# Routing tokens tile by tile inside the cross-attention projection, 5 and 6 weight homes, and filler products, in a one-core decoder block

## What is computed

```python
def rmsnorm(x, g):
    y = xf * lax.rsqrt(jnp.mean(xf * xf, axis=-1, keepdims=True) + EPS)
    return (y * g).astype(x.dtype)

x = x + hybrid_mixer(rmsnorm(x, mix_norm_g[l]), ...)            # 512 x 1024
x = x + cross_attention(rmsnorm(x, xatt_norm_g[l]), mem_n, ...) # ends with o @ w_xo
x = x + hierarchical_moe(rmsnorm(x, ffn_norm_g[l]), ...)
return rmsnorm(x, final_norm_g)

def hierarchical_moe(h, ...):
    g_logits = t @ w_group + b_group                    # 4 groups, the best one is taken
    g_idx = jnp.argmax(g_logits, axis=-1)
    e_logits = (t @ w_router + b_router)                # 4 experts of that group, the best two
    top_v, top_i = lax.top_k(softmax(e_sel), 2)         # their weights, renormalised
    hid = silu(t @ w_gate[e]) * (t @ w_up[e])           # 1024 -> 256
    out = out + (hid * combine[e]) @ w_down[e]          # 256 -> 1024
```

## Time and profile before

| | us |
|---|---|
| median of 3 runs (744.43 to 748.34) | 744.91 |
| the profiled execution | 748.57 |
| its span in the trace | 746.8 |
| PE busy | 695.0 |
| PE in the chain that ended last | 89% of the span |

### The profile page before, as it was taken

The page is one execution under the profiler, slowest core; times in us unless marked ns, Lnnn a source line. Parts: engine busy times, 40 slices in busy tenths (PEclk is TensorE's granted clock), DMA queues, the critical chain, the costliest instruction groups (busy, mean ns, idle before and its releaser), DMA issues.

```text
span 746.8 us, 8354 instructions
## 1 busy us (share of the span) xinstructions
PE 695.0 (93%) x3388; PEld 332.9 (45%) x3388; DVE 279.4 (37%) x647; ACT 147.9 (20%) x305; POOL 69.5 (9%) x94
## 2 busy tenths in 40 slices
PE   5999999999999899999999999999946999999975
PEld 4744444454455565444444446444432333333322
DVE  3108699925143564313220016312241821212147
ACT  3010431004262343311000014201110010101002
POOL 2000090520100000000000000000010010100122
PEclk9999999999999999999999999999966999999988
DMA  8703330303130203300029311200196999999552
GB/s 296 271 0 113 113 112 2 112 2 113 57 117 23 91 1 113 114 0 1 0 83 367 112 59 54 112 30 28 64 355 207 323 351 389 369 388 352 204 185 112
DMA packets 65715, 108.21 MB, mean 145 GB/s; under 512 B 5401, under 2 KB 40461, under 8 KB 65677
## 3 DMA queue, kind: packets, MB, share of 16 engines
q1 hardware_dynamic: 62796, 97.19, 37.3%
q0 software_dynamic: 2880, 10.49, 3.9%
HBM read 98.23 MB, written 9.44 MB: 144 GB/s over the span
## 4 chain that ended last, share of the span: by engine, by line
PE 89%; DVE 5%; ACT 2%; DMA 1%; another core or an unknown queue 1%; issue 1%; POOL 1%; DVEq 0%; POOLq 0%
PE bank L1742 25%; PE bank L2043 15%; PE bank L1614 12%; PE bank L1752 6%; PE bank L1642 6%; PE bank L1774 2%; PE bank L2116 2%; PE bank L1788 2%; PE bank L2096 2%; PE bank L1560 2%; PE bank L1596 2%; PE bank L1983 2%; PE bank L1959 1%; PE bank L1859 1%; PE bank L1884 1%
## 5 line engine op out<-in xcount | busy, mean ns | idle before, releaser
L1742 PE MATMUL bank<-hT,W 128*128 128x512 f32 x368 | 159.7, 593 | 0.9 <-DVE hT L1006 0.9
L2043 PE MATMUL bank<-W,n_sb 128*128 128x512 f32 x256 | 111.5, 594 | 0.7 <-ACT n_sb L974 0.7
L1742 PEld LDWEIGHTS bank<-hT,W 128*128 128x128 f32 x368 | 69.4, 190 | 87.5 <-issue 86.0
L2043 PEld LDWEIGHTS bank<-W,n_sb 128*128 128x128 f32 x256 | 48.1, 190 | 59.8 <-issue 58.3
L1614 PE MATMUL bank<-W,A 128*32 128x512 f32 x528 | 73.2, 614 | 1.5 <-DVE A L1160 1.5
L1319 DVE SCALAR_TENSOR_TENSOR A<-A,pc 128x511 f32<-128x511 f32 (+29 forms) x60 | 51.6, 860 | 2.0
L1642 PE MATMUL bank<-Dn,A 128*32 128x512 f32 x384 | 46.5, 627 | 5.1 <-ACT A L775 5.1
L649 POOL TENSOR_TENSOR rstd<-ss,mhalf 128x1 f32<-128x1 f32 x14 | 7.7, 549 | 376.5 <-DVE ss L990 376.5
L1614 PE MATMUL bank<-hT,A 128*32 128x512 f32 x96 | 42.3, 594 | 0.0
L1507 DVE TENSOR_TENSOR x_sb<-x_sb,bank 128x512 f32<-128x512 f32 x16 | 11.0, 687 | 79.7 <-PE bank L2043 79.7
L1614 PEld LDWEIGHTS bank<-W,A 128*32 128x32 f32 x528 | 19.4, 113 | 43.2 <-issue 41.0
(11 more groups left out here) (294 smaller groups left out, 829.0 us busy)
## 6 DMA issues: line engine op xcount, KB each, us to landing
Dn<-in_w_down_dram SPq DMA_DIRECT2D x16, 1024.0 KB, 12.3
W<-in_w_gate_dram SPq DMA_DIRECT2D x11, 1024.0 KB, 7.7
W<-in_w_up_dram SPq DMA_DIRECT2D x11, 1024.0 KB, 11.0
W<-in_w_in_dram SPq DMA_DIRECT2D x5, 2048.0 KB, 12.2
W<-in_w_xkv_dram SPq DMA_DIRECT2D x4, 2048.0 KB, 8.0
y_dram<-A SPq DMA_DIRECT2D x10, 512.0 KB, 10.9
W<-in_w_out_dram SPq DMA_DIRECT2D x2, 2048.0 KB, 7.8
W<-in_w_xq_dram SPq DMA_DIRECT2D x2, 2048.0 KB, 9.0
```

Source lines behind the costliest of these rows:

```text
L1742: mm = nc.tensor.matmul(bank[0:w, 0:n], lhs, src[:, c, 0:n], start=c == 0, stop=c == DC - 1)
L2043: mm = nc.tensor.matmul(PS[k % 4][:, :], src[:, c, t * P:(t + 1) * P], W[:, (n_load + n) % SLOTS, c, :], start=first and j == 0, stop=last ...
```

## The change

It does five things.

1. **Routing by token tiles.** `logits_of` is gone. The new `experts_pe` runs the last projection itself and puts, between the chunks of the next half, the turning of the raw `x_sb` half (`turn_half`), half of the logits (`logits_half`, tokens stationary and the router's 20 columns moving), the places (`position`) and the token numbers (`tokens`) of earlier tiles. DVE does `choose` and `place` for tile t-1 between its additions. The normalisation factor is applied to the logits and not to the turned rows, and ACT scales the rows for `n_dram` (`scaled_rows`).
2. **Homes.** Gate and up have 5 homes (`hT` is no longer one), down has 6 (the two new ones in `hT`).
3. **SP's order.** The gate load of the third expert stands ahead of the store of the last tile and its up load behind it. The loads for the two new down homes wait for the first gather. The stores of `y_dram` move from SP to POOL. The final gain is loaded earlier. The gathers at the end go to `W` slot 0 and `n_sb`, the final norm to `W` slot 3.
4. **Products of constants.** `keep_busy` multiplies two constant tiles (128x128 by 128x512) into a free bank: 2 and 1 at the start, 2, 6 and 1 between the routing of the last tile and pass 0.
5. **Start.** Tile 1 of x is loaded ahead of `w_if`, and its mean is taken before tile 0 is turned.

```diff
-GU_HOMES, DN_HOMES = 6, 4
+GU_HOMES, DN_HOMES = 5, 6
...
+            sp.dma_start(fgain, ...).then_inc(router_in, 16)
             for t in range(ST - 1):
                 store_rows(t)
             sp.wait_ge(*freed(14))
-            load_gate_up(sp, TAKEN[2])
+            load_gate(sp, TAKEN[2])
             store_rows(ST - 1)
+            load_up(sp, TAKEN[2])
             load_gate_up(sp, TAKEN[3])
             load_gate_up(sp, TAKEN[4])
-            sp.wait_ge(lgt_ps, ST)
-            load_gate_up(sp, TAKEN[5])
+            sp.wait_ge(logits_ps, ST)
+            sp.wait_ge(xg_in[0], 16)
+            for e in TAKEN[:DN_HOMES]:
+                if DN_HOME[e] >= SLOTS:
+                    load_down(sp, e)
...
+            def store_pass(p):
+                pool.wait_ge(y_act, p + 1)
+                pool.wait_ge(y_dve, p + 1)
+                nc.gpsimd.dma_start(y_rows[p], ysb[:, p % 2]).then_inc(y_stored[p % 2], 16)
             for p in range(NP):
                 ...
+                if p >= 4:
+                    store_pass(p - 4)
...
+            def choose(t):
+                n = NORM0[3] + t
+                dve.wait_ge(logits_ps, t + 1)
+                dve.wait_ge(rstd_done, n + 1)
+                link(nc.vector.scalar_tensor_tensor(out=logits[:, t], in0=PS[6][...],
+                                                    scalar=rstd[:, n:n + 1], in1=rbias, ...))
+                nc.vector.tensor_tensor(above, across_rows(sets), across_cols(sets), ALU.is_ge)
+                link(nc.vector.tensor_tensor(beats, ..., ALU.is_gt))
+                link(nc.vector.copy_predicated(beats, low, above))
+                link(nc.vector.tensor_reduce(rank, beats, AX_X, ALU.add))
+                link(nc.vector.tensor_tensor(chosen[:, t], rank, limit, ALU.is_lt))
+                nc.vector.tensor_tensor(pickedb[:, t]..., ALU.mult).then_inc(picked_done, 1)
+                nc.vector.tensor_tensor(tokg16[:, t], ...).then_inc(pick_done, 1)
+            def place(t):
+                dve.wait_ge(pos_ps, t + 1)
+                link(nc.vector.tensor_reduce(rowm16[:, t], PS[7][...], AX_X, ALU.min))
+                nc.vector.tensor_tensor(pick[:, t], ..., ALU.is_equal).then_inc(pick_done, 1)
+            for t in range(ST):
+                if t:
+                    turn_evac(dve, 3, t - 1, 1, PS[5], hT, R_FFN)
+                    full_mean(t - 1)
+                    choose(t - 1)
+                add_half(t, 0)
+                turn_evac(dve, 3, t, 0, PS[4], hT, R_FFN)
+                if t:
+                    place(t - 1)
+                first_mean(t)
+                add_half(t, 1)
...
+        def keep_busy(n, bank):
+            for _ in range(n):
+                nc.tensor.matmul(bank[:, :], identf[:, :], scanmask[:, :], start=True, stop=True)
...
+            for t in range(ST):
+                first, middle, rest = range(2), range(2, 5), range(5, DC)
+                project_some(8, 14, xoT, 2 * t, first, last=False)
+                if t:
+                    turn_half(t - 1, 1)
+                project_some(8, 14, xoT, 2 * t, middle, first=False, last=False)
+                if t:
+                    logits_half(t - 1, 1)
+                project_some(8, 14, xoT, 2 * t, rest, first=False)
+                project_some(8, 14, xoT, 2 * t + 1, first, last=False)
+                turn_half(t, 0)
+                if t:
+                    position(t - 1, range(t))
+                project_some(8, 14, xoT, 2 * t + 1, middle, first=False, last=False)
+                logits_half(t, 0)
+                if t == ST - 1:
+                    position(t, range(t))
+                    for u in range(t):
+                        tokens(u)
+                project_some(8, 14, xoT, 2 * t + 1, rest, first=False)
+            turn_half(ST - 1, 1)
+            logits_half(ST - 1, 1)
+            keep_busy(2, PS[3])
+            position(ST - 1, [ST - 1])
+            count()
+            tokens(ST - 1)
...
             pe.wait_ge(over_done, 1)
+            keep_busy(6, PS[3])
             turn_pass(0)
+            keep_busy(1, PS[3])
...
+            pe.wait_ge(consts, 6)
+            keep_busy(2, PS[1])
             pe.wait_ge(mix_in, 16)
-            pe.wait_ge(consts, 5)
...
             turn_tile_pe(0, 0, n_sb)
+            keep_busy(1, PS[1])
             pe.wait_ge(ff_in, 16)
```

More of the change, by code:

```diff
@@ L249, in build @@
         onesb = srow[:, 384:448].bitcast(BF16)
-        lower = srow[:, 448:464].rearrange("p (i j) -> p i j", i=4)
+        lower = srow[:, 448:464].bitcast(I32).rearrange("p (i j) -> p i j", i=4)
         ebase = srow[:, 464:480]
@@ L610, in experts_gathers @@
                                              in_offset=bass.IndirectOffsetOnAxis(ap=token_of[:, p:p + 1], axis=0)).then_inc(xg_in[p % 2], 16)
+                if p >= 4:
+                    store_pass(p - 4)
+            for p in range(NP - 4, NP - LATE):
+                store_pass(p)
             def final_root(t):
@@ L1052, in experts_dve @@
+            turn_evac(dve, 3, ST - 1, 1, PS[5], hT, R_FFN)
+            full_mean(ST - 1)
+            choose(ST - 1)
+            place(ST - 1)
+            dve.wait_ge(token_ps, 1)
+            nc.vector.tensor_copy(token_of, PS[4][:, 0:NP]).then_inc(token_done, 1)
             link(nc.vector.tensor_reduce(gtop, gl, AX_X, ALU.max))
             nc.vector.tensor_tensor(gexp, gl, over_last(gtop, NG), ALU.subtract).then_inc(soft_in, 1)
-            rank(gl, grank)
-            link(nc.vector.tensor_scalar(ghot, grank, 0.0, None, ALU.is_equal))
@@ new lines, in experts_pe, with turn_half, logits_half, position @@
+        def experts_pe(pe, project_some):
+            def turn_half(t, k):
+                pe.wait_ge(x1_done, 8 + 2 * t + k + 1)
+                if t:
+                    pe.wait_ge(turn_sb, TURN0[3] + 2 * t + k - 1)
+                for c in range(4):
+                    mm = nc.tensor.transpose(PS[4 + k][:, c * P:(c + 1) * P], x_sb[:, t, (4 * k + c) * P:(4 * k + c + 1) * P], identf[:, :])
+                mm.then_inc(turned, 1)
+            def logits_half(t, k):
+                pe.wait_ge(turn_sb, TURN0[3] + 2 * t + k + 1)
+                for c in range(4 * k, 4 * k + 4):
+                    mm = nc.tensor.matmul(PS[6][:, t * (NG + EX):(t + 1) * (NG + EX)], hT[:, c, t * P:(t + 1) * P], wgr[:, c, :],
+                                          start=c == 0, stop=c == DC - 1)
+                if k:
+                    mm.then_inc(logits_ps, 1)
+            def position(t, tiles):
+                if t in tiles:
+                    pe.wait_ge(picked_done, t + 1)
+                else:
+                    pe.wait_ge(pick_done, 2 * t)
+                for u in tiles:
+                    mm = nc.tensor.matmul(PS[7][:, t * EX:(t + 1) * EX], onesb if u < t else before, pickedb[:, u],
+                                          start=u == 0, stop=u == t)
+                if t in tiles:
+                    mm.then_inc(pos_ps, 1)
+            def count():
+                for u in range(ST):
+                    mm = nc.tensor.matmul(PS[5][:, 0:EX], onesb, pickedb[:, u], start=u == 0, stop=u == ST - 1)
+                mm.then_inc(pos_ps, 1)
+            by_pass = PS[4][:, 0:NP].rearrange("p (g j) -> p g j", g=NG)
+            def tokens(t):
+                pe.wait_ge(pick_done, 2 * t + 2)
@@ L2061, in project_out @@
                         turn_tile_pe(stage, t - 1, nA)
-                    if t >= 2 and stage == 3:
-                        for u in ([t - 2] if t < ST else [t - 2, t - 1]):
-                            logits_of(u)
             pe.wait_ge(ho_step, 4)
```

213 lines of the change are left out of this document (105 added, 108 removed).

## The result

| | before | after |
|---|---|---|
| median | 744.91 us | 741.21 us |
| lowest to highest of five | 744.43 to 748.34 | 740.72 to 742.70 |
| profiled execution | 748.57 (span 746.8, mean clock 0.972) | 742.70 (span 739.2, 0.981) |

The ratio is 0.9946, interval 0.9925 to 0.9966. The sign was right and the size less than half of the forecast. The time is inside the range of 729 to 742, but at its slow end, where my price for late weights (740) stood; none came late, so that it is inside is luck.

What follows compares the result with a forecast made beforehand. PE, with 89% of the chain of waits, was taken to bound the kernel, apart from 29.6 us between projection and pass 0. Terms +5.8 - 10.9 - 2.5 - 1.4 = -9.0 us from the median 744.91 gave 735.9 us, range 729 to 742.

Steps and rivals of the forecast that it cites:

- late weights: Rival, chance 0.12: weights become the bound from about pass 8 on; price 4 us, giving 740.
- part 1: Projection: routing work put between its chunks makes it longer, +5.8 us (4.2 to 7.4), a half tile of logits costing 0.68.
- the six fillers: Ahead of turning pass 0's rows: they run from 8.8 to 16.5 us behind the projection and decide over the gather.
- part 2: From the projection's end to pass 0's first product: 18.7 us where it was 29.6, -10.9 us (16.9 to 20.5).
- the gain of a full clock in pass 0: First 64 records of pass 0: the clock is up by then, 9.60 becomes 7.07, -2.5 us.
- the base of the sum: Starting time: profiled execution 748.57 less 9.0 is 739.6; the median, 744.91, is 3.7 lower, giving 735.9 us.
- Part 4: Transfers in the passes: homes and stores on POOL cost PE nothing, 20 us in hand; 0, bound +5.
- PE does not wait for DVE inside the projection: DVE's work there was costed at nothing; the slower rival, chance 0.03, had PE waiting, 15 us added, 751.
- Two filler products cost nothing: Ahead of the last tile's places: two fillers take 1.7 us and end at 4.5, before DVE's `choose` at 4.6.
- Part 3: Kernel start: products behind the input gates begin at 28.7 instead of 30.1, -1.4 us (+1.7 to -2.1).
- The end wait: Rival, chance 0.09: the wait ahead of the last `down_pass` goes, some 7 us less, 729.
- The last tile's landing: In `n_dram`, expected 6.8 us behind the projection; rival, chance 0.08: it lands at 10.9, giving 738.

Runs made afterwards that it cites:

- no_routing_filler: Changed kernel without its 2, 6 and 1 filler products at the last tile's routing, start fillers kept; 734.68 us beside 738.59 for before, ratio 0.9943.
- zero_products: Changed kernel with a second product, 20 columns of zeros on the same stationary chunk, behind each router logits product; 742.89 us where the changed kernel has 734.39.
- before_again: Kernel before, unchanged, run again for a second trace; 738.46 us beside 738.59, ratio 0.9996.
- before_third: Kernel before, unchanged, run a third time for another trace; 745.60 us beside 745.99, ratio 0.9995.
- start_only: Kernel before with only the change's start: second tile of x ahead of first weights, start fillers, one mean earlier; 738.43 us beside 738.59, ratio 0.9991.
- filler_only: Kernel before with only six filler products during the gather of pass 0's rows and one behind their turning; 736.42 us beside 738.59, ratio 0.9970.
- homes_back: Changed kernel with before's homes (six gate and up, four down), end rows gathered to two weight slots; 745.36 us beside 745.20 for before, ratio 1.0000.
- after_third: Changed kernel, unchanged, run again on a chip without the wait near the end; 734.39 us beside 738.12 for before, ratio 0.9946.

## Why the prediction was wrong in size

**What failed.** The mechanism held for the most part; four sizes did not. The price of a half tile of logits (part 1), the place of the six fillers behind the projection (part 2), the gain of a full clock in pass 0, and the base of the sum, one long execution. Part 4 named a reason that was wrong, though its term of 0 came out.

**What was right.** The order of things behind the projection: the clock falls in the routing, pass 0 comes back to full rate, and at first sight the filler and not the gather stands in front of it (7.38 us of line 1626 up to 561.35, while the gathered rows of no_routing_filler were there 15.6 us behind the projection). PE does not wait for DVE inside the projection, no weights are late in the passes, and line 1857 starts at 28.60 where 28.8 was foretold.

**Part 1, the price of a half tile of logits.** I took 0.085 a record, between 64-column records and turned chunks, and gave as reason that the moving side shrinks. The changed kernel has 0.80 for 8 records, zero_products 0.11 a record. The nearest row was the turned chunk at 0.109: same stationary side. The part came to 66.2 - 59.0 = +7.2 and not +5.8. In the chain of after the seven halves take 5.6 us (I had 4.8). The projection's own 128 records take 56.3, cut into pieces, where they took 55.4 in three runs (I had 55.5). Places and token numbers take 1.3 (I had 1.6). The Trainium skill's rule (TensorE: Matmul & The Clock Gate, LDWEIGHTS), stationary columns divided by 1.2 in ns, gives 107 ns for 128 columns. The 0.10 and 0.11 measured here agree with it, and an estimate by it would have been +7.0.

**Part 2, the tail.** I had 18.7 us for it; the traces of after have 19.7, 19.5, 21.2 and 19.4, so -9.9, -10.0, -8.4 and -10.2 (29.6 before). "Two filler products cost nothing" failed in the trace of after: they took 2.92 us and not 1.7, since the clock had fallen under them at 547.7, and DVE was ready about 1 us before they ended. Leaving them out brought 0.7 us in a trace and 0.3 in the median, the latter inside the spread. The larger miss is where the six stand: I had them from 8.8 to 16.5 us behind the projection. In the four traces they start at 10.5, 10.6, 10.9 and 9.4 and end between 17.6 and 19.3. Their own length, 7.1 to 8.4 us, lies on both sides of my 7.7. In after the steps ahead of them are each late: the last half's addition starts at 0.4 and not 0, the logits end at 3.7 and not 2.8, the two fillers at 6.6 and not 4.5. Behind the six it is 1.8 us to the first product and not 2.2.

**Pass 0 at full clock.** -2.5 came from 9.60 us in one trace. before_again and before_third have 8.50 and 8.49; against those it is -1.4. start_only has 9.62, so of four traces with this pass 0 two are long and two short. filler_only, which removes this and little else, measured -2.2 with an interval from -1.3 to -3.1, so it decides nothing between them.

**Part 3, the start.** -1.6 in the first pair of traces for my -1.4. The way there was the one foretold, but the first products began at 10.54 and not 11.6. Alone on the chip it was -0.2, with an interval from -1.8 to +0.4; and the start of before varies by 1.3 us (30.22 in the first trace, 28.94 in filler_only, whose start is that of before).

**Part 4, transfers.** The term of 0 was right, its reason was not. I said that the kernel had 20 us in hand and that homes cost nothing. The 20 us were a sum over all passes; at the down load of pass 6 the kernel before had 0.4 to 0.6. homes_back shows that with the old homes the same routing brings nothing at all, since that load is then 2.9 us late and PE behind it is at half clock. My rival "weights become the bound" (0.12) was the right mechanism for a kernel with the old homes, and the 5/6 homes, for which I had found no use, are what keeps it away. What SP's new order of loads and the stores on POOL do by themselves was not measured.

**The base.** I summed differences against an execution of 748.57 and took the sum from the median, 744.91, as if the excess of 3.7 us lay elsewhere. Part of it lay in what the change alters: its pass 0 was 1.1 us longer than in the other two traces, its start 0.5 to 0.7.

**The sum again**, from another pair, before_third and after_third: start -1.5 (476.52 to 475.04), projection +7.2, behind it -8.4, pass 0 -1.4: -4.1 up to pass 1, and 0 in the passes. The time outside the span is 1.7 to 1.8 us in before and 2.0 to 2.1 in all but two of the 21 executions of after: +0.3. That gives -3.8; measured were -3.7 to -4.0 in four comparisons. The agreement is better than three and four traces deserve. With the other traces of after the tail is up to 1.8 us shorter, and before_third is 1.1 us under its own median while after_third is 0.5 under its own. Of the 5.3 us that are missing, 1.4 are the projection, about 1.3 the tail (the mean of the four), about 1.1 pass 0, 0.3 the time outside; some 1.2 are in none of these, and the runs leave open whether they are in the start or in where the clock's low stretches fall.

**The rivals.** The end wait stayed, in before and after alike, and hides nothing. The last tile's landing was late by 1 us against my 6.8, which mattered only without filler.

## What to carry to other kernels

A sum read from one execution holds for that one: where its time is above the median, take the same stretches from a second trace before subtracting from the median, above all those at a low clock. Price a small product by the nearest row with the same stationary side: 20 moving columns cost here what 128 did, 0.11 us. And filler in front of data that have landed costs what it saves; it is free only inside a wait that is longer than it is. And when work is moved nearer to its loads, undo the buffer change on paper too: what looks idle in the diff may be what pays for the rest. Read the cover of each load from its own landing and use, and not from a sum over all of them.

## What the hardware showed beyond that

- The granted clock fell while PE was never idle, in zero_products at 545.5 behind thin records: 18 records in the microsecond from 544 on, at 1.00, and 0.51 from 547 to 549.
- A low stretch at 227 to 232 us, in the same products of both kernels, comes in some executions and not in others, and is worth 1.6 us (5.36 against 3.72 for the same 16 records). start_only has such a stretch at 254 to 257 instead.
- Where before takes 745 us, a copy on ACT and one on DVE were kept for 4 to 6 us during a burst of eight indirect gathers, though neither reads what is gathered. Four gathers held back, it was gone, and the kernel 8.1 us faster; that was tried on one chip. The same instructions run without it elsewhere: from the start of the last gate products to the end it is 45.1 us in before_third and 38.3 in before_again, which is about the difference between their 744.5 and 738.0.
